# Twelve expert groups a layer: the down products as seven half-size products, the splitting shared out anew, and q's low parts ahead of k's norm

## The reference

```python
def peer_ffn(x, w_query, sub_keys, u_tab, v_tab):
    ...
        gate = jax.nn.softmax(sv, axis=-1)
        u = u_tab[eidx]
        act = jax.nn.gelu(jnp.einsum('thkd,td->thk', u, xc), approximate=False)
        w = gate.astype(act.dtype) * act
        vv = v_tab[eidx]
        return jnp.einsum('thk,thkd->td', w, vv)
```

## Time and profile before

| | us |
|---|---|
| median of three runs | 3792.05 |
| the profiled execution | 3792.64 |
| its span, first to last instruction | 3790.8 |
| TensorE (PE) busy | 3741.3 (99%) |
| PE weight load (PEld) busy | 3091.1 (82%) |
| VectorE (DVE) busy | 2252.6 (59%) |
| GpSimd (POOL) busy | 2245.9 (59%) |
| ScalarE (ACT) busy | 852.0 (22%) |
| HBM traffic | 553 MB, 146 GB/s over the span |

### The profile page before, as it was taken

One profiled execution on the slowest core, in us unless ns is written; L12 is line 12 of the kernel. 1 busy time (PEld: TensorE's weight loads), 2 busy tenths in 40 slices (PEclk: granted clock), 3 DMA queues, 4 the chain that ended last, 5 costly groups with the idle time before them and its releaser, 6 DMA issues.

```text
span 3790.8 us, 52844 instructions
## 1 busy us (share of the span) xinstructions
PE 3741.3 (99%) x18624; PEld 3091.1 (82%) x18624; DVE 2252.6 (59%) x3825; ACT 852.0 (22%) x1409; POOL 2245.9 (59%) x1148
## 2 busy tenths in 40 slices
PE   8999999999999999999999999999999999999998
PEld 7778888888888888888877788888888888888887
DVE  7545998985777422222375469989767773222224
ACT  1551234441111111011015412344411110101110
POOL 6445554337877666666564455543377776666664
PEclk9999999999999999999999999999999999999999
DMA  4123245886555333333221223468864553333332
GB/s 151 67 70 107 98 149 180 249 240 245 189 204 188 127 117 124 130 111 122 89 102 64 81 100 104 147 194 245 254 233 187 188 199 121 124 122 122 113 120 77
DMA packets 230076, 554.97 MB, mean 146 GB/s; under 512 B 10048, under 2 KB 141376, under 8 KB 181440
## 3 DMA queue, kind: packets, MB, share of 16 engines
q1 hardware_dynamic: 47968, 337.14, 25.0%
q10 hardware_dynamic: 181984, 216.17, 17.2%
HBM read 446.32 MB, written 106.95 MB: 146 GB/s over the span
## 4 chain that ended last, share of the span: by engine, by line
PE 95%; DVE 3%; POOL 1%; issue 1%; ACT 0%; DMA 0%; SPq 0%; DVEq 0%; POOLq 0%; ACTq 0%
PE bank L1195 29%; PE bank L1196 29%; PE bank L1197 29%; PE bank L1523 2%; PE bank L1524 2%; POOL part_l L422 1%; PE bank L1320 1%; PE bank L1483 1%; PE bank L1308 1%; PE bank L1299 0%; DVE X L796 0%; PE bank L1374 0%; PE bank L1300 0%; DVE X L798 0%; DVE rs L778 0%
## 5 line engine op out<-in xcount | busy, mean ns | idle before, releaser
L422 POOL TENSOR_TENSOR part_l<-landing,part_h 128x1024 fp32r<-128x1024 f32 x632 | 1637.8, 2595 | 496.8 <-ACT part_h L638 454.0
L432 POOL TENSOR_SCALAR part_h<-landing 128x1024 fp32r<-128x1024 f32 x508 | 611.6, 1204 | 1008.4 <-PE bank L1197 769.8
L1195 PE MATMUL bank<-XTh,part_h 128*128 128x512 f32 (+1 forms) x2688 | 1048.5, 390 | 2.5 <-DVE XTl L806 2.4
L1196 PE MATMUL bank<-XTl,part_h 128*128 128x512 f32 (+1 forms) x2688 | 1034.7, 385 | 0.0
L1197 PE MATMUL bank<-XTh,part_l 128*128 128x512 f32 (+1 forms) x2688 | 1034.4, 385 | 0.0
L1195 PE MATMUL bank<-part_h,Wh 128*128 128x512 f32 x2048 | 797.0, 389 | 0.9 <-POOL part_l L422 0.9
L1196 PE MATMUL bank<-part_l,Wh 128*128 128x512 f32 x2048 | 796.8, 389 | 0.0
L1197 PE MATMUL bank<-part_h,Wl 128*128 128x512 f32 x2048 | 796.7, 389 | 0.0
L1143 DVE TENSOR_TENSOR X<-X,bank 128x512 f32<-128x512 f32 x480 | 307.8, 683 | 549.8 <-PE bank L1197 549.8
L1195 PEld LDWEIGHTS bank<-XTh,part_h 128*128 128x128 f32 x2688 | 505.7, 188 | 101.7 <-DVE XTl L806 3.4
L1197 PEld LDWEIGHTS bank<-XTh,part_l 128*128 128x128 f32 x2688 | 505.6, 188 | 101.5
(11 more groups left out here) (171 smaller groups left out, 3393.3 us busy)
## 6 DMA issues: line engine op xcount, KB each, us to landing
landing<-stream SPq DMA_DIRECT2D x316, 1024.0 KB, 4.8
dense_gates<-spill ACTq DMA_DIRECT2D x32, 2048.0 KB, 9.3
gate<-dense_gates ACTq DMA_DIRECT2D x64, 1024.0 KB, 4.8
early_acts<-early ACTq DMA_DIRECT2D x144, 256.0 KB, 2.5
acts_in<-early_acts ACTq DMA_DIRECT2D x36, 1024.0 KB, 7.5
LNP<-ln ACTq DMA_DIRECT2D x4, 1024.0 KB, 5.1
X<-x SPq DMA_DIRECT2D x4, 512.0 KB, 7.4
keyT<-keys ACTq DMA_DIRECT2D x2, 1024.0 KB, 4.8
```

What stands on the lines that cost most here:

```text
L422: nc.gpsimd.tensor_tensor(halves(part_l[s], h), halves(landing[s], h), halves(part_h[s], h).bitcast(F32), ALU.subtract).then_inc(split.sem, 1)
L432: nc.gpsimd.tensor_scalar(halves(part_h[s], h), halves(landing[s], h), 1.0, 0.0, ALU.mult, ALU.add).then_inc(high_part.sem, 1)
L1195: nc.tensor.matmul(dst, sth, mvh, start=first, stop=False)
L1196: nc.tensor.matmul(dst, sth, mvl, start=False, stop=False)
```

## The change

**Seven products.** The down products of twelve groups a layer (groups 18 to 29, SG = 12) become seven products of half size. W V is cut in 2 x 2 blocks: W by 256 tokens and 256 experts, V by 256 experts and 512 channels. The sums of blocks of W and of V are those of Winograd's form of Strassen's method. One of the seven is 2 token blocks x 2 chunks x 3 = 12 matmuls of 512 columns.

TensorE's order in such a group (`seven_group`) is: half an up product of the next group, P1, P2, P3, P5, the other half, P4, P7, P6. A product waits for its low parts of V and for the sum of the product two before it in `seven_added`, since two pairs of banks alternate:

```diff
+                def seven_products(k, par, i):
+
+                    pe.wait_ge(v_low.sem, v_low.at(l, 7 * k + (i + 1)))
+                    pe.wait_ge(seven_added.sem, seven_added.at(l, 7 * k + (i - 1)))
+                    vh, vl = unit(part_h, i), unit(part_l, i)
+                    for j in range(2):
+                        ts = slice(j * P, (j + 1) * P)
+                        for a in range(2):
...
+                            ins = product(bank[4 + 2 * ((par + i) % 2) + j][:], wh, wl, vh[:, a, :], vl[:, a, :],
+                                          a == 0, a == 1)
+                    ins.then_inc(seven_done.sem, 1)
+                def seven_group(k, par):
...
+                    up(0, 2 * k + S_FIRST, 0, bank_free)
+                    pe.wait_ge(y_added.sem, y_added.at(l, 4 * EG))
+                    pe.wait_ge(s_low.sem, s_low.at(l, 2 * k + 2))
+                    for i in (P1, P2, P3, P5):
+                        seven_products(k, par, i)
+                    up(1, 2 * k + (S_FIRST + 1), 1, bank_free)
+                    for i in (P4, P7, P6):
+                        seven_products(k, par, i)
```

```diff
+                def gate_cross(a, par, p):
...
+                    nc.vector.tensor_tensor(a21, bank[c][:, HALF:S], gate[0][:, HALF:S, c], ALU.mult)
+                    nc.vector.tensor_tensor(a11, a11, gate[0][:, 0:HALF, c], ALU.mult).then_inc(w_full.sem, 1)
+                    dve.wait_ge(w_full.sem, w_full.at(l, CG * a + (CG * EG + 2 * p + 1)))
+                    nc.vector.tensor_tensor(sum_of[par][:, S3, p, :], a11, a21, ALU.subtract)
+                def seven_group(k, par, last):
+
+                    def table_sum(n, out, left, right):
+                        nc.vector.tensor_tensor(block_of(*out), block_of(*left), block_of(*right),
+                                                ALU.subtract).then_inc(t_added.sem, 1)
...
+                    sum_lows(k, par, 1)
+                    dve.wait_ge(v_landed[1].sem, v_landed[1].at(l, 16 * k + 16))
+                    dve.wait_ge(v_low.sem, v_low.at(l, 7 * k + (P1 + 1)))
+                    table_sum(1, b11, b12, b11)
+                    dve.wait_ge(t_added.sem, t_added.at(l, 4 * k + 1))
+                    table_sum(2, b12, b22, b12)
...
+                        gate_cross(k + 1, next_par, 0)
+                    dve.wait_ge(v_low.sem, v_low.at(l, 7 * k + (P3 + 1)))
+                    dve.wait_ge(t_added.sem, t_added.at(l, 4 * k + 2))
+                    table_sum(3, b22, b22, b11)
+                    gate_chunk(k + 1, 1)
+                    if not last:
+                        sums(k + 1, next_par, 0)
...
+                    add_seven(k, par, P1)
...
+                        raw_lows(k + 1, next_par, 0)
+                    add_seven(k, par, P2)
+                    if not last:
+                        sum_lows(k + 1, next_par, 0)
+                    add_seven(k, par, P3)
+                    dve.wait_ge(t_added.sem, t_added.at(l, 4 * k + 3))
+                    table_sum(4, b21, b22, b21)
+                    add_seven(k, par, P5)
...
+                        gate_cross(k + 1, next_par, 1)
+                    gate_chunk(k + 1, 3)
+                    if not last:
+                        sums(k + 1, next_par, 1)
+                    add_seven(k, par, P4)
...
+                        raw_lows(k + 1, next_par, 1)
+                    add_seven(k, par, P7)
+                    add_seven(k, par, P6)
```

**ScalarE** makes all highs of these groups, of U (`up_high`) and V (`down_high`), in halves of 128 x 1024:

```diff
+                def seven_group(k, par, last):
...
+                    act.wait_ge(*multiplied(0))
+                    act.wait_ge(used.sem, used.at(l, ups))
+                    act.wait_ge(v_landed[0].sem, v_landed[0].at(l, 16 * k + 16))
+                    down_high(P1)
+                    down_high(P2)
+                    activate(k + 1, 0, None)
+                    act.wait_ge(v_landed[1].sem, v_landed[1].at(l, 16 * k + 16))
+                    down_high(P3)
+                    activate(k + 1, 1, ups + 1)
+                    act.wait_ge(*added(1))
+                    down_high(P5)
...
+                    up_high(k, 1, 0, multiplied(P1 + 1))
+                    if not last:
+                        raw_highs(k + 1, next_par, 0)
+                        sum_highs(next_par, 0)
+                    up_high(k, 1, 1, multiplied(P2 + 1))
+                    act.wait_ge(*multiplied(P3 + 1))
+                    act.wait_ge(*added(4))
+                    down_high(P4)
+                    act.wait_ge(*multiplied(P5 + 1))
+                    act.wait_ge(*added(2))
+                    down_high(P7)
+                    activate(k + 1, 2, None)
+                    act.wait_ge(*added(3))
+                    down_high(P6)
+                    activate(k + 1, 3, ups + 2)
...
+                        up_high(k + 1, 0, 0, multiplied(P4 + 1))
+                        raw_highs(k + 1, next_par, 1)
+                        sum_highs(next_par, 1)
+                    fetch(k + (EG + 2), 0, False)
+                    if not last:
+                        up_high(k + 1, 0, 1, multiplied(P7 + 1))
```

**POOL** makes only the lows there, in a fixed order:

```diff
+            def seven_lows(l, k):
...
+                up_lows(0)
+                for i in (P1, P2, P3, P5):
+                    down_low(i)
+                up_lows(1)
+                for i in (P4, P7, P6):
+                    down_low(i)
```

**SyncE** loads the V pieces of these groups into two buffers of their own, `vraw`, each when the last of its lows is made (P4's for the first, P6's for the second):

```diff
+                with sp.Fori(0, SG - 1) as k:
+                    up_piece(k + 1, 0)
+                    up_piece(k + 1, 1)
+                    sp.wait_ge(v_low.sem, v_low.at(l, 7 * k + (P4 + 1)))
+                    down_piece(k + 1, 0)
+                    sp.wait_ge(v_low.sem, v_low.at(l, 7 * k + 7))
+                    down_piece(k + 1, 1)
```

**q and k.** q's low parts stand ahead of the tables and k's norm:

```diff
                 for g in range(GROUPS):
                     if g == GROUPS // 2:
-                        gained(1)
-                        dve.wait_ge(kv_copied.sem, kv_copied.at(l, 2))
-                        norm_heads(HEADS, NORMED, TB * HEADS, k_turn, root_out.at(l, 2))
                         for h in range(2):
                             dve.wait_ge(q_high.sem, q_high.at(l, h + 1))
...
+                        gained(1)
+                        dve.wait_ge(kv_copied.sem, kv_copied.at(l, 2))
+                        norm_heads(HEADS, NORMED, TB * HEADS, k_turn, root_out.at(l, 2))
                     dve.wait_ge(*y_ready(l, g))
```

More of the change, by code:

```diff
@@ new lines, in end_highs, with up_high @@
+                def end_highs(g, end, half):
+                    for c in (2 * half, 2 * half + 1):
+                        act.wait_ge(w_full.sem, w_full.at(l, CG * g + c + 1))
+                        nc.scalar.copy(end_h[end][:, c, :], bank[c][:]).then_inc(w_high.sem, 1)
+                def up_high(k, s, h, ready):
+                    act.wait_ge(landed[s], l * (8 * NS) + (16 * k + (8 * S_FIRST + 16)))
+                    act.wait_ge(*ready)
+                    w = slice(h * PIECE // 2, (h + 1) * PIECE // 2)
+                    nc.scalar.copy(part_h[s][:, w], landing[s][:, w]).then_inc(u_high.sem, 1)
@@ L1175, in _ @@
-                dve.wait_ge(y_added.sem, y_added.at(l, 4 * NG - 4))
+                dve.wait_ge(used.sem, used.at(l, P_UV))
+                for p in range(2):
+                    gate_cross(0, 0, p)
+                    gate_chunk(0, 2 * p + 1)
+                    sums(0, 0, p)
+                    raw_lows(0, 0, p)
+                    if p == 0:
+                        dve.wait_ge(y_added.sem, y_added.at(l, 4 * EG - 4))
+                        sum_lows(0, 0, p)
+                    add_up(EG - 1, p, P_UV + 2 * p + 2, False)
@@ new lines, in _ @@
+                dve.wait_ge(y_added.sem, y_added.at(l, 4 * EG))
+                for i in range(4):
+                    ins = nc.vector.memset(acc[i][:], 0.0)
+                ins.then_inc(acc_zero.sem, 1)
+                with dve.Fori(0, SG // 2 - 1) as m:
+                    for par in range(2):
+                        seven_group(2 * m + par, par, False)
+                seven_group(SG - 2, 0, False)
+                seven_group(SG - 1, 1, True)
+                gather_seven()
+                for half in range(2):
+                    for c in (2 * half, 2 * half + 1):
+                        gate_chunk(NG - 1 - EG, c)
+                    end_lows(1, half)
+                    if half == 0:
+                        dve.wait_ge(acc_step.sem, acc_step.at(l, 8))
+                    add_up(EG, half, S_UV + 2 * half + 2, False)
@@ L1558, in weighed_rows @@
                         ts, w = slice(tb * P, (tb + 1) * P), slice(c * S, (c + 1) * S)
[L1559 to L1565 removed]
+                        ins = product(dst[:], wh[:, c, ts], wl[:, c, ts], ph[:, w], pl[:, w], c == 0, c == CG - 1)
@@ L1566, in down @@
+                    return ins
+                def down(group, wh, wl, half, n, slot, first=None):
+                    pe.wait_ge(w_low.sem, w_low.at(l, CG * group + CG))
                     for s in range(2):
-                        if not first:
```

(6 more changed lines are left out.)

349 lines of the change are left out of this document (268 added, 81 removed).

## The result

The changed kernel takes 3823.69 us in the median of 4 runs (3817.43 to 3824.81) against 3791.85 us: ratio 1.008, interval 1.0067 to 1.0092. It is 32 us slower; 3852 was forecast, with 3755 to 3885 as the range. The profiled execution took 3824.81 us, its span is 3823.0 us.

What follows compares the result with a forecast made beforehand. Matmul pace on PE was taken as the bound. From 3792.6, fewer matmuls take 65.3; waits for P1's sum add 81.6, the clock 40, q and k 3.3: 3852 us, range 3755 to 3885.

Steps and rivals of the forecast that it cites:

- the rival without the clock's fall: PE's stall in the seven-product groups comes, but the clock doesn't fall: 3812, ±8; chance 0.12.
- What goes: Down products of 24 groups: 84 matmuls instead of 96 each, 288 fewer, saving 65.3 us, all on the path.
- The chain in one group: DVE's `table_sum`s wait for POOL's lows at the port; P1's sum comes at 19.8, PE waits from 16.3.
- step 1: At the group's start, DVE's `sum_lows` finds POOL busy with P1's low and runs from 3.7 to 4.8.
- The price of the wait: PE's wait before P3: idle about 3.3, 3.4 us lost a group, 24 x 3.4 = +81.6 us.
- the race: Step 4 of the group's chain: P5's low on POOL starts 0.2 us ahead of DVE's `table_sum` 3.
- The clock: PE's clock falls behind three in four of the groups' stalls, at 2.2 us: +40 us, bounds 0 and 62.
- q and k: Same work reordered, q's lows earlier: +1.7 us a layer, together +3.3, between -9.4 and +5.
- The sum: Whole kernel: 3792.6 - 65.3 + 81.6 + 40 + 3.3 = 3852 us.
- That of the won race: Rival: `table_sum` 3 gets in ahead of P5's low; wait 1.4, clock holds, 3764; chance 0.18.
- that without a stall: Rival: some operations taken as exclusive are not, DVE has P1 added by 15.2: 3731; chance 0.11.
- The second wait: Rival: PE also waits at P5 for P2's sum or for U's low, 1.5 us more each: 3888; chance 0.10.

Runs made afterwards that it cites:

- the kernel with no waits in the groups: Changed kernel with `table_sum` 3 behind P3's addition, P1's sum ahead of the block sums, P2's ahead of the raw lows, q's lows behind k's norm: 3727.53 us.
- The kernel with this edit alone: The kernel before with q's low parts put ahead of k's norm, nothing else: 3794.75 us, ratio 1.0007.
- the shortened lows: Changed kernel with P2's, P3's and P5's low parts made for only 256 of 1024 elements: 3730.23 us, ratio 0.9836.
- the shortened low: Changed kernel with POOL making P5's low parts for only 256 of 1024 elements of a partition: 3773.05 us, ratio 0.9949.
- one reduction: Changed kernel with one unused reduction of a bank added on DVE behind `table_sum` 3 in 22 of 24 groups: 3881.85 us, ratio 1.0236.
- With two: Changed kernel with two unused reductions of a bank added on DVE behind `table_sum` 3 in 22 of 24 groups: 3885.19 us, ratio 1.0245.

## Why the prediction was right, and where it was off

The direction and its mechanism were right, and the forecast was 28 us too high, nearly all in one term. The measured 3823.7 lies just outside the band of the forecast itself (3825 to 3885) and above that of the rival without the clock's fall (3804 to 3820): the clock fell, but in fewer groups than I took.

- *What goes.* 65.3 us; the kernel with no waits in the groups is 64.4 us faster than the one before (3791.89 - 3727.53). Right.
- *The chain in one group.* Counted from 1491.94, `table_sum` 1 ends at 8.3 (8.1 forecast), `table_sum` 2 at 11.6 (11.45), `table_sum` 3 comes at 13.1 (12.9), P5's low starts at 12.7 (12.7) and ends at 15.1 (15.05), P1's sum is there at 19.7, P3 starts at 19.8 (19.8). One detail of step 1 was the other way round: DVE's `sum_lows` came 0.2 us ahead of P1's low, not behind; `table_sum` 1 ends at the same time in either order, within 0.2 us.
- *The price of the wait.* Recorded idle 3.3 us, as forecast. The group lasts 44.4 instead of 44.2 us: the two starts around the wait are 3.69 us apart, so 3.46 are lost there, and the next matmul starts 0.33 later instead of 0.227 (the rows at 1508.03, 1511.72 and 1512.05). 22 groups have the wait, not 24: in the last of a layer DVE wins the race and has no block sums to make, and P1's sum comes in time. I had taken 1.5 us off the last and given them to the first, whose wait is no longer than the others'. 22 x 3.6 = 79 against 81.6.
- *The clock.* The term that was mis-sized: I took 40 us, three stalls in four at 2.2 us each. It fell in 9 of 22, at some 1.7 us each. In the profiled run the ten distances of the first layer add up to 453.3 us and those of the second to 448.7, against 444.1 at 44.41 each: 13.8 us, some 15 with the last wait's. The step that failed is the likeness to the 3.00 us wait of the earlier trace rows, which had another of 1.31 just before it; mine stand alone. That this is the reason, no run shows. The rival without any fall (3812, 0.12) had that argument, and the truth lies between the two, a third of the way up.
- *q and k.* 6.2 us instead of 4.7: +3.0 for 3.3 forecast. The kernel with this edit alone shows the wait; its time rose by 2.4. DVE's table products and k's square took the waits for POOL.
- *The sum.* 3792.6 - 65.3 + 79 + 15 + 3 = 3824.3, measured 3824.8 in the profiled run.
- *The rivals.* That of the won race, at 3764, was built and gave 3768.8; that without a stall was put at 3731, and the shortened lows gave 3730.2, though by less work at the port and not by an operation that stays out of it. The second wait didn't come. DVE lost the race by 0.38 to 0.53 us in the 22 groups and won it by 0.14 in the last of each layer.

The Trainium skill's page "SBUF — State Buffer" (section "SBUF: two separate sides") has the pair of ports as an exclusive lock for a whole instruction. By that rule the shortened low must shorten DVE's instruction by as much; the trace agrees, 1.67 against 1.68 us.

What stays open: why of waits of the same 3.3 us some lower the clock and others don't. They come in rows of one to three groups with a fall, with others without one between. In the profiled run of the changed kernel the granted clock falls between 0.6 us ahead of P3's start and 1.6 us behind it, so not at a fixed time after the wait began, and the one group of 47.3 us has a lower stretch twice as long as the others. No run here varied anything else than the wait's length.

## What to carry to other kernels

Fewer matmuls pay only as far as the other engines' order keeps up, and shares don't tell that: DVE was busy for 73% and all its work fitted, yet one instruction at the wrong place in its queue cost 81 us (3823.7 against 3742.3) and turned a gain of 50 us into a loss of 32. When VectorE gets operations with two SBUF inputs beside a busy GpSimd, write the two queues down against each other, charge each such operation with a whole instruction of the other engine, and keep them out of the stretch between a product and the addition that frees its banks.

## What was not expected of the hardware

- A wait of 1.6 us on PE never lowered the clock, one of 3.3 us in 8 or 9 of 22 cases, one of 3.9 in all 22. The kernels with 3.9 and with 4.5 us wait have the same distance of groups, 47.8 us. The trace shows why the 0.6 us more cost nothing. With one reduction the granted clock falls 0.8 us ahead of P3's start and rises 6.0 behind it (P3 at 1566.91). With two it falls 2.1 us ahead and rises 4.8 behind (P3 at 1567.97). The lower stretch is as long, and 1.2 us less of it lie behind the wait, on matmuls; at half pace that is 0.6 us.
- DVE work ahead of an instruction that waits for the port was free: two reductions of 0.64 us each (1.28 together), in 22 groups, cost nothing, and the instruction's 3.10 us became 1.91.
- Behind a wait even at full clock two matmuls together lose about 0.1 us beside the idle time (0.33 us between starts instead of 0.227).
